# A narrow expert gathers its successor's tokens amid its own units, the last unit's rows are turned between down products, and results are returned in two rounded passes

## The reference

```python
D_MODEL, SEQ = 1024, 256
N_EXPERTS, TOP_K = 8, 2
D_FF_EXPERT = 7 * D_MODEL // 2          # 3584

def swiglu(x, w1, w3, w2):
    return (jax.nn.silu(x @ w1) * (x @ w3)) @ w2

def moe_swiglu(x, router_w, w1, w3, w2):
    t = x.reshape(B * S, D)
    logits = (t @ router_w).astype(jnp.float32)
    top_v, top_i = lax.top_k(logits, TOP_K)
    gates = jax.nn.softmax(top_v, axis=-1)
    combine = jnp.sum(jax.nn.one_hot(top_i, N_EXPERTS) * gates[..., None], axis=1)
    out = jnp.zeros_like(t)
    for e in range(N_EXPERTS):
        out = out + combine[:, e:e + 1] * swiglu(t, w1[e], w3[e], w2[e])
    return out.reshape(B, S, D)
```

## Time and profile before

| | us |
|---|---|
| median of 3 runs | 2407.71 (2405.58 to 2408.87) |
| the profiled execution | 2408.15 |
| its span, first to last instruction | 2406.0 |
| TensorE busy | 2189.7 (91%) |
| TensorE weight loads busy | 1743.8 (72%) |
| VectorE busy | 1407.4 (58%) |
| ScalarE busy | 1141.1 (47%) |
| GpSimd busy | 1286.9 (53%) |
| mean granted clock of TensorE | 0.952 |

### The profile page before, as it was taken

One profiled execution on the slowest core, in us unless ns is written; L12 is line 12 of the kernel. 1 busy time (PEld: TensorE's weight loads), 2 busy tenths in 40 slices (PEclk: granted clock), 3 DMA queues, 4 the chain that ended last, 5 costly groups with the idle time before them and its releaser, 6 DMA issues.

```text
span 2406.0 us, 26806 instructions
## 1 busy us (share of the span) xinstructions
PE 2189.7 (91%) x10576; PEld 1743.8 (72%) x10576; DVE 1407.4 (58%) x1744; ACT 1141.1 (47%) x1156; POOL 1286.9 (53%) x555
## 2 busy tenths in 40 slices
PE   8988699989888699999999999999899996887997
PEld 7577488865675577777777777888677773746997
DVE  1774533345744576777767676343367675455665
ACT  1143234321431475766667674333366672534554
POOL 0334145402440497988989796455389892204453
PEclk9999899989999799999999999999999998978999
DMA  8210075523000598999989897455489894204550
GB/s 293 105 36 1 16 257 181 181 97 130 36 1 1 202 367 310 340 338 323 368 294 368 294 362 261 174 180 195 156 288 363 296 366 146 105 35 158 210 193 35
DMA packets 208105, 485.11 MB, mean 202 GB/s; under 512 B 9168, under 2 KB 13008, under 8 KB 206928
## 3 DMA queue, kind: packets, MB, share of 16 engines
q1 hardware_dynamic: 207952, 483.02, 55.6%
HBM read 481.96 MB, written 1.05 MB: 201 GB/s over the span
## 4 chain that ended last, share of the span: by engine, by line
PE 82%; DVE 11%; ACT 3%; issue 2%; SPq 1%; DMA 1%; POOL 0%; DVEq 0%; ACTq 0%
PE bank L920 20%; PE bank L922 19%; PE bank L921 19%; PE bank L549 11%; PE bank L741 5%; PE bank L556 3%; DVE b_arena L1244 2%; DVE b_arena L1238 1%; DVE e_lo L1696 1%; PE bank L1016 1%; PE bank L702 1%; ACT e_hi L2050 1%; DVE b_X L1238 1%; PE bank L1131 1%; DVE b_arena L1241 1%
## 5 line engine op out<-in xcount | busy, mean ns | idle before, releaser
L2655 POOL TENSOR_TENSOR e_lo<-b_ring,e_hi 128x512 fp32r<-128x512 f32 (+3 forms) x407 | 1135.0, 2811 | 594.1 <-ACT e_hi L2050 594.1
L1696 DVE TENSOR_TENSOR e_lo<-b_ring,e_hi 128x1536 fp32r<-128x1536 f32 (+1 forms) x403 | 770.1, 1912 | 483.3 <-ACT e_hi L2050 479.2
L2050 ACT ACTIVATE e_hi<-b_ring 128x2048 fp32r<-128x2048 f32 (+1 forms) x407 | 776.5, 1911 | 396.0 <-PE bank L922 358.4
L920 PE MATMUL bank<-e_hi,e_xh 128*128 128x512 f32 (+1 forms) x1200 | 481.4, 401 | 35.4 <-issue 25.1
L922 PE MATMUL bank<-e_hi,e_xl 128*128 128x512 f32 (+1 forms) x1200 | 469.0, 391 | 0.0
L921 PE MATMUL bank<-e_lo,e_xh 128*128 128x512 f32 (+1 forms) x1200 | 468.7, 391 | 0.0
L920 PEld LDWEIGHTS bank<-e_hi,e_xh 128*128 128x128 f32 x1200 | 228.2, 190 | 103.8 <-issue 55.6
L920 PE MATMUL bank<-e_hi,e_th 128*128 128x512 f32 x688 | 271.4, 394 | 2.4 <-DVE e_tl L1700 2.4
L922 PE MATMUL bank<-e_hi,e_tl 128*128 128x512 f32 x688 | 268.4, 390 | 0.0
L921 PE MATMUL bank<-e_lo,e_th 128*128 128x512 f32 x688 | 268.2, 390 | 0.0
L922 PEld LDWEIGHTS bank<-e_hi,e_xl 128*128 128x128 f32 x1200 | 228.1, 190 | 48.5
(11 more groups left out here) (211 smaller groups left out, 2413.2 us busy)
## 6 DMA issues: line engine op xcount, KB each, us to landing
b_ring<-in_moe_w SPq DMA_DIRECT2D x168, 2048.0 KB, 8.2
b_ring<-in_w_in SPq DMA_DIRECT2D x15, 2048.0 KB, 9.1
b_ring<-in_ffn_w SPq DMA_DIRECT2D x15, 2048.0 KB, 7.8
b_ring<-in_w_up SPq DMA_DIRECT2D x12, 2048.0 KB, 8.0
b_ring<-in_w_down SPq DMA_DIRECT2D x6, 2048.0 KB, 9.2
b_ring<-in_w_o SPq DMA_DIRECT2D x4, 2048.0 KB, 7.9
b_gain<-in_gains SPq DMA_DIRECT2D x7, 1024.0 KB, 4.8
b_ring<-in_w_out SPq DMA_DIRECT2D x2, 2048.0 KB, 8.4
```

Source lines behind the costliest of these rows:

```text
L920: e.matmul(out, ah, bh, start=first, stop=False)
L1696: e.tensor_tensor(lo[:, 0:at], raw[:, 0:at], r32(hi[:, 0:at]), ALU.subtract).then_inc(lo_dve.sem)
L2050: return e.activation(out, x, ACT.Copy)
L2655: e.tensor_tensor(lo[:, at:], raw[:, at:], r32(hi[:, at:]), ALU.subtract).then_inc(lo_pool.sem)
```

## The change

Five things change, in all engines' lists alike:

- A narrow expert gathers its successor's first tile in two halves, behind the turns of its third and fourth unit, and turns the selection behind those of the fifth; ScalarE and VectorE copy these at fixed places of the following unit. The gathered tokens go to the block of `e_xh` and `e_xl` that the running expert doesn't read. A wide expert still gathers at its end. The selection on VectorE goes to the second unit's turn, behind the rest of the turned rows.
- The last unit's turns stand between the two down pieces of the unit before (one tile, with `e_th` and `e_tl` used in turn) or inside the second of them (two tiles; the dense layer too).
- The shares are not multiplied into the selection. TensorE turns `e_P` alone and makes a column of the shares with two fp32 products of one column (`turn_picks`), and ScalarE and VectorE multiply the results by that column as they leave PSUM.
- ScalarE writes the rounded result `e_yh` (both halves) and VectorE what is left, `e_yl`; the return products are eight rounded ones instead of four fp32 ones. The second tile of a wide expert still returns in fp32.
- GpSimd's part of the first two pieces of an expert is two eighths instead of four.

```diff
 def steps_of(widths, tiles):
-        out += [("w1", u, 0)] * (u < n) + [("T", u - 1, 0)] * (u > 0)
+        out += [("w1", u, 0)] * (u < n) + [("T", u - 1, 0)] * (0 < u < n)
...
         if u:
-            out += [("d", u - 1, h) for h in range(widths[u - 1] // 256)]
+            down = [("d", u - 1, h) for h in range(widths[u - 1] // 256)]
+            if u == n - 1:
+                down.insert(1 if tiles == 1 else len(down), ("T", u, 0))
+            out += down
+def turned_at(tiles, s, u):
+    return u % 2 if tiles == 1 else s
+def block_of(ex, s):
+    return (ex + s) % 2

 TensorE
+            def turn_picks(ex, s, b):
+                e.wait_ge(*pick[s](ex))
+                turn(bank[b], [e_P[s][:, t, :] for t in range(2)])
+                sums(bank[b][:, 256:257], [(e_P[s][:, t, :], comb[:, t, ex:ex + 1]) for t in range(2)]).then_inc(pt_turn[s].sem)
             def finish(ex):
-                give_back(ex, 0, e_GT[0][ex % 2], [e_y[:, half(n)] for n in range(2)], 4)
+                e.wait_ge(*y_dve[0](ex))
+                e.wait_ge(*y_act[0](ex))
+                pt = e_PT[0][ex % 2]
                 for t in range(2):
                     for n in range(2):
-                        e.matmul(bank[first + 2 * t + n][:, :], gt[:, tok(t)], y[n], start=True, stop=True).then_inc(back[s].sem)
+                        b = bank[4 + 2 * t + n]
+                        e.matmul(b[:, :], pt[:, tok(t)], e_yh[:, half(n)], start=True, stop=False)
+                        e.matmul(b[:, :], pt[:, tok(t)], e_yl[:, half(n)], start=False, stop=True).then_inc(back[0].sem)
-                def tail():
-                    if more:
-                        gather(ex + 1, 0, (0, 1))
-                        e.wait_ge(tl_out.sem, 2 * (unit + 6) + 2 // tiles)
-                        turn_shares(ex + 1, 0, 2)
+                def aside(kind, u, hf):
+                    if ex and (kind, u, hf) == ("w1", 0, 1):
+                        finish(ex - 1)
+                    if more and tiles == 1 and kind == "T" and u in (2, 3):
+                        gather(ex + 1, 0, u - 2, 2 * u - 3)
+                    if more and tiles == 1 and kind == "T" and u == 4:
+                        turn_picks(ex + 1, 0, 6)
+                    if more and tiles == 2 and kind == "T" and u == 6:
+                        for g in range(2):
+                            gather(ex + 1, 0, g, g)
+                        e.wait_ge(*tl_out(unit + 6))
+                        turn_picks(ex + 1, 0, 2)
 TensorE, two tiles: the last unit's turns
+                            if tiles == 2 and u == n - 2 and hf == 1:
+                                turn_h(s, n - 1)

 VectorE
             def selected(ex, s):
                 for t in range(2):
-                    r, j = rank[:, t, ex:ex + 1], C("iota")[:, 128 * s:128 * s + 128]
-                    ts(e_P[s][:, t, :], j, r, None, ALU.is_equal)
-                    ins = ts(e_G[s][:, t, :], j, r, comb[:, t, ex:ex + 1], ALU.is_equal, ALU.mult)
+                    ins = ts(e_P[s][:, t, :], C("iota")[:, 128 * s:128 * s + 128], rank[:, t, ex:ex + 1], None, ALU.is_equal)
+                def aside(kind, u, hf):
+                    if ex and (kind, u, hf) == ("w3", 0, 0):
+                        add_back(ex - 1, 0, 4)
+                    if more and kind == "T" and u == 1:
+                        selected(ex + 1, 0)
+                    if more and tiles == 1 and (kind, hf) == ("w3", 0) and u in (3, 4):
+                        gathered(ex + 1, 0, u - 3, 2 * u - 5)
+                    if more and tiles == 1 and (kind, u, hf) == ("w3", 5, 0):
+                        picks(ex + 1, 0, 6)
 VectorE, end of an expert
-                    e.tensor_copy(e_h[0][:, :], bank[6][:, :]).then_inc(y_dve[1].sem)
-                e.tensor_copy(e_y[:, half(0)], bank[4][:, :]).then_inc(y_dve[0].sem)
+                    ts(e_h[0][:, :], bank[6][:, :], e_gate[1][0][:, 0:1], None, ALU.mult).then_inc(y_dve[1].sem)
+                for n in range(2):
+                    e.wait_ge(*y_act[0](ex, n))
+                    stt(e_yl[:, half(n)], bank[4 + n][:, :], e_gate[0][ex % 2][:, 0:1], r32(e_yh[:, half(n)]),
+                        ALU.mult, ALU.subtract).then_inc(y_dve[0].sem)

 ScalarE, end of an expert
-                if tiles == 2:
-                    copy(e_h[1][:, :], bank[7][:, :]).then_inc(y_act[1].sem)
-                copy(e_y[:, half(1)], bank[5][:, :]).then_inc(y_act[0].sem)
+                for n in range(2):
+                    f(e_yh[:, half(n)], bank[4 + n][:, :], ACT.Copy, 0.0, e_gate[0][ex % 2][:, 0:1]).then_inc(y_act[0].sem)
+                if tiles == 2:
+                    f(e_h[1][:, :], bank[7][:, :], ACT.Copy, 0.0, e_gate[1][0][:, 0:1]).then_inc(y_act[1].sem)

 GpSimd
-                    split_rest(MOE_P + 42 * ex + i, 4 if ex and i < 2 else 6)
+                    split_rest(MOE_P + 42 * ex + i, 6)
```

More of the change, by code:

```diff
@@ L927, in take_piece, with gated, turn_h @@
                 return e_hi[p % NH], e_lo[p % NH]
-            def gated(widths, at, unit, tiles, first=None, after_w1=None, tail=None):
+            def gated(widths, at, unit, tiles, first=None, aside=None, where=(0, 1)):
                 n, p = len(widths), at
-                for kind, u, hf in steps_of(widths):
+                def turn_h(s, u):
+                    e.wait_ge(h_mul.sem, 2 * (unit + u) + (s + 1) * 2 // tiles)
+                    turn(bank[2 + s], [e_h[s][:, tok(c)] for c in range(widths[u] // 128)]).then_inc(h_turn.sem, 2 // tiles)
+                for kind, u, hf in steps_of(widths, tiles):
                     w = widths[u]
@@ L938, in gated @@
                         for s in range(tiles):
[L939 to L942, removed]
+                            if tiles == 1 or u < n - 1:
+                                turn_h(s, u)
+                        if aside:
+                            aside(kind, u, hf)
                         continue
@@ L1057, in experts @@
                 e.wait_ge(*flag_out(0))
-                gather(0, 0, (0, 1))
-                turn_shares(0, 0, 2)
+                for g in range(2):
+                    gather(0, 0, g, g)
+                turn_picks(0, 0, 2)
                 for ex in range(NE):
@@ L1715, in gated @@
-                        continue
-                    if p + 2 < ends:
-                        split_rest(p + 2, 4 if tail and p + 2 >= at + 42 else 6)
-                    if add_last and (kind, u, hf) == ("w3", 0, 0):
-                        add_last()
-                    if kind == "w3" and hf == 1:
-                        for s in range(tiles):
-                            e.wait_ge(*piece(p))
-                            e.wait_ge(silu.sem, 2 * (unit + u) + (s + 1) * inc)
-                            tt(e_h[s][:, 0:w], e_h[s][:, 0:w], bank[2 + s][:, 0:w], ALU.mult).then_inc(h_mul.sem, inc)
@@ L1725, in gated @@
-                    p += 1
+                    else:
+                        if p + 2 < ends:
+                            split_rest(p + 2, 6)
+                        if kind == "w3" and hf == 1:
+                            for s in range(tiles):
+                                e.wait_ge(*piece(p))
+                                e.wait_ge(silu.sem, 2 * (unit + u) + (s + 1) * inc)
+                                tt(e_h[s][:, 0:w], e_h[s][:, 0:w], bank[2 + s][:, 0:w], ALU.mult).then_inc(h_mul.sem, inc)
+                        p += 1
@@ L1848, in experts @@
                 selected(0, 0)
-                gathered(0, 0, (0, 1))
-                shares(0, 0, e_GT[0][0], 2)
+                for g in range(2):
+                    gathered(0, 0, g, g)
+                picks(0, 0, 2)
                 for ex in range(NE):
@@ L2307, in split_round, with gated @@
                 copy(hi, raw).then_inc(w_hi.sem)
[L2309 to L2311 removed]
+            def gated(widths, at, unit, tiles, ends, aside=None):
+                p, inc = at, 2 // tiles
+                for kind, u, hf in steps_of(widths, tiles):
                     w = widths[u]
```

174 lines of the change are left out of this document (94 added, 80 removed).

## The result

The kernel after takes 2415.05 us (median of 7 runs, 2414.49 to 2418.41) beside 2407.71 for the one before: 1.0034 times as long, 95% interval 1.0022 to 1.0045. It is slower by 7.3 us where 12.3 less were forecast. Its profiled span is 2416.2 against 2406.0, 22.5 us more than the 2393.7 that the sum gave. (The profiled execution is the slowest of the seven, 3.4 over the median.)

A forecast was written before the change was run, and what follows sets the result against it. TensorE, busy 91% of 2406.0 us, was taken as the bound, with the holes in its stream. Terms -11.2 - 4.0 + 1.7 + 3.4 - 1.4 - 0.8 + 1.2 - 1.2 = -12.3 gave 2395.4 us; range 2388 to 2405.

The forecast's parts named there:

- The holes at five taken branches: Between experts at the branch into the narrow arm: holes unchanged, taken as 0, bounds 0 and +13.7 us.
- a hole over 4: Sign at the branch after an expert's last product: 2.6 to 3.0 us expected; over 4 means wrong towards slower.
- The eighth return: After the last expert: start 1.3 us later, about 1.3 back as additions follow sooner, taken as 0.
- Return in two passes: Return products at an expert's end: 3.44 us becomes 1.84, gain 1.60 each, seven inside the stream, -11.2.
- Picks: Selection turns for seven successors and the wide expert's second tile: two one-column fp32 products add 0.43 each, +3.4 us.
- Selection and regular hole: Six narrow experts: last-unit hole 1.17 falls to 0.51, -4.0 us; late-piece hole returns at the last down piece, +1.7.
- Last turns: Turns between down products: idle 1.64 in the last expert saves 1.4 us, idle 0.81 in the dense layer saves 0.8.
- the second down piece suffices as cover: Previous unit's second down piece, 2.8 us, covers copy and rest of the last turned rows, some 1.8.
- Wide expert: Its end: two ScalarE passes ahead, +1.2 us; its entry: shorter wait for the selection, -1.2, bounds 0 and -2.
- The branch is read somewhat late: Rival at the five branch holes: half the upper bound, +1.2 each, +6, giving 2401.4 us; chance 11%.
- It is read fully late, and the clock goes with it: Rival at the five branch holes: +13.7 us and +7 of slow clock, net +8.4, giving 2416.1; chance 5%.
- The hole was VectorE's after all: Rival: better order closes the five holes and their slow clock, -20.5 us more, giving 2374.9; chance 7%.

The follow-up runs named there:

- mark given early: Kernel after with gather and turns at the expert's end and the fourth load held, plus the narrow expert's VectorE mark given before returned rows are split: 2383.70 us.

## Why the prediction was wrong

**The step that failed** is "The holes at five taken branches", taken at 0 because "the nearest row is the first expert's entry". Its lead was indeed 1.5, and the new lead came out at 1.4. What failed is the branch's duration that was lent with the lead: 4.03 at that entry, 6.1 to 6.4 at the five branches, since a weight load is now issued 1.3 us ahead of each. At the entry the load was issued 5.3 ahead. It kept the DMA engines full for another 1.6 us (813.2 to 814.8), and the fetch started only as it ended; with no load under way such a branch takes 3.3 to 3.5 in the kernel before.

```profile
q1 hardware_dynamic: 164, 0.66, 100.3%
```

Measured: 10.8 us at the five holes (2.2, 2.4, 1.9, 2.1 and 2.2 more than before). By the recorded branches and leads 6.6 of them are the shorter lead and 4.2 the longer branch; at the branch of 4.03 that was lent, the shorter lead would have cost nothing. The row that contradicted the loan stood in the same group, 5.28 against 4.03: I didn't ask where its difference came from. The sign given ahead, a hole over 4 "makes me wrong towards slower", is what came.

**What no term held**: the second holes, 5.6 + 3.3 = 8.9 beyond the regular spacing. They are the same wait on the following 16384 bytes of code: in the traces they stand 4 and 16 instructions of TensorE's queue behind the arms' first, and they went when eighty instructions moved the code.

**The eighth return**, "about 1.3 back": the start is late by 1.5 (the last product at 2012.55, the first return product at 2015.30), and only 0.3 comes back: at the clock's lower level most of the eight take 0.43 each. From the last product to the next stage's first it is 25.7 us, 24.4 before: +1.3.

```profile
2012.55 0.39 PE L940 MATMUL bank<-e_hi,e_tl 128*128 128x512 f32 x1
2015.30 0.77 PE L1049 MATMUL bank<-e_yh,e_PT 128*128 128x512 f32 x1 [2.37 <-DVE e_yl L1292]
```

Together 10.8 + 8.9 + 1.3 = 21.0 of the 22.5. The other 1.5 is left over and wasn't taken apart. I put it down to the clock, which I had left at 0 with 4 either way: a slow stretch behind the dense layer is 10 us long instead of 17 (some 3 less), and the longer holes cost it again: over the experts the clock is at its lower level for 55 us of the span, where it was 31.

**The terms that held.** *Return in two passes*: eight products in 1.82 (1095.90 to 1097.72), the next without idle, against 3.44.

```profile
1095.90 0.39 PE L1049 MATMUL bank<-e_yh,e_PT 128*128 128x512 f32 x1
1096.13 0.39 PE L1050 MATMUL bank<-e_yl,e_PT 128*128 128x512 f32 x1
...
1097.72 0.39 PE L938 MATMUL bank<-e_hi,e_xh 128*128 128x512 f32 x1
```

*Picks*: 1179.14 to 1179.73 is 0.59 against 0.14 for the shares, +0.45 (forecast 0.43).

```profile
1179.14 0.38 PE L574 MATMUL bank<-b_cst,e_P 128*128 128x128 f32 x2
1179.36 0.50 PE L567 MATMUL bank<-b_moe_comb,e_P 128*128 128x1 f32 x4
1179.73 0.48 PE L938 MATMUL bank<-e_hi,e_xh 128*128 128x512 f32 x1
```

*Selection and regular hole*: 1.17 has become 0.51 (1062.24 to 1062.75), and the regular hole is back behind the moved turns, 0.50 at the last down piece. *Last turns*: no idle behind them in expert 7 or in the dense layer, where the earlier trace rows had 1.64 and 0.81. That the second down piece suffices as cover is shown from the other side by the kernel with the turns put back, seven idles of 1.63 and 11.1 us. *Wide expert*: the end costs 2.41 from the last product to the first returned where it was 1.38 (+1.0, forecast 1.2), the entry 3.56 where it was 4.87 (-1.3, forecast -1.2).

```profile
1739.00 0.39 PE L940 MATMUL bank<-e_hi,e_tl 128*128 128x512 f32 x1
1741.41 1.62 PE L1058 MATMUL bank<-e_h,e_PT 128*128 128x512 f32 x2 [2.03 <-ACT e_h L2113]
```

The terms left in the kernel with gather and turns at the end were to give -12.6, and -12.1 was measured. That supports the sum but doesn't prove it to half a microsecond, since the kernel has changes that no term of it holds: its five holes are 0.7 longer together, and its entry to the wide expert 1.3 shorter.

**The rivals.** "The branch is read somewhat late", 11%, came true as far as it went: +6 on five holes was its price, and the shorter lead is 6.6. (Half the upper bound of 2.7 is 1.4 a hole, not 1.2; measured 1.3.) It was set aside by the first entry's row. "It is read fully late, and the clock goes with it" gave 2416.1 and 2415.05 was measured, but not by its way: the lead was 1.4 and no product waited for a branch read late. Its condition, more than 3.4 us a hole beyond before, wasn't met either (2.2). That its time was right is luck: the second holes and the longer branches made it up. "The hole was VectorE's after all" was dismissed as a whole, and is half right: under the branch lies a mark of VectorE's, at 0.9 in the kernel before and, behind the new splitting of the returned rows, at 2.19 in the one after. It is hidden while branches last 5 us and binds when they are short. The Trainium skill's rule that I cited (Runtime: NRT & Kernel Launch, Instruction fetch mechanics: a taken branch waits for the transfer of its target) agrees with every trace here: no taken branch ends less than 2.3 us behind the start of a packet of code. The same section of the Trainium skill calls the crossing of a 16 KiB boundary mostly hidden. Right behind a branch, with a load under way, it isn't: 5.8 and 3.5 us in the kernel after, and 2.8 and 1.6 in the same two experts with the load held.

## What to carry over

A branch's price is its fetch's, less the lead, and the fetch starts late when a bulk load was issued ahead of it. Where control flow is taken on the critical engine, look at what the load queue does in the 5 us ahead, and let the next load wait until all the code is there. Here such a wait was worth 29, 20 and 12 us in three kernels. Where the next load was let go at the branch already, it gained 12 in one kernel and cost 6 in another. A change that evens out a pipeline moves its loads too, since they start when buffers come free: follow the issue times past every branch. And when a duration is lent from one row to another place, ask what else was under way at both; two rows that differ by 1.3 us for the same instruction are a question, not a scatter.

## What was not expected of the hardware

- With no load issued in the 7 us ahead, the fetch starts 0.9 to 1.6 us behind the branch and the branch ends 2.3 to 3.0 later. A load of 2 MB issued 1.3 us ahead moves the start to 3.5 to 3.9, one 4.2 ahead to 2.7 to 3.0. One issued 0.5 us behind the branch doesn't move it, though it is ahead of the fetch's record; it delays the second fetch, which is recorded 6.5 to 7.8 us behind the branch and not 4.0 to 5.1. The instruction packet itself takes about 1.0 us at either time (12.4% of 16 engines for 0.5 us after, 11.7% in the kernel before with the load held): it waits, it isn't slowed. The Trainium skill (DMA: Bandwidth & Descriptors, Queues, rings and completion order) says that an engine takes its queues in turn, packet by packet. The runs show up to 2.9 us of waiting, and whether that rule accounts for it is open: neither the engine that carries the fetch nor smaller loads were tried.
- Unexecuted code is not free: 80 instructions of it, placed so that they moved the crossings, took 6.9 us off.
- Of TensorE's clock: at the five branches it fell from its upper to its lower level (0.50 in the rows) around all nineteen holes of 3.7 us and more, around some of those of 2.2 to 3.1, and around none of the nineteen of 0.8 to 1.4. Elsewhere it was not so: a hole of 3.95 behind the wide expert (mark given early) and one of 3.56 at its entry (kernel after) left it at its upper level.
